# A hybrid two-layer trunk step on one core: wide routing, late modulation blocks, attention results by feature, split queries and keys

## The reference

```python
mc = split(silu(c_ctx) @ mod_w[l] + mod_b[l], 6)       # shift, scale, gate, shift2, scale2, gate2; ms: same with c
h  = rms_norm(x, norm1_w[l]) * (1 + scale) + shift
# layer 0: qa, ka, va, qb, ff, fb, ib, gb = split(h @ even_w_in)
#   8 query heads of 64 on 2 key heads; context tokens: dense attention with a sink;
#   latent tokens: rope, 128 cached keys and a band of +-128, with a sink
#   HGRN2 recurrence in both directions, 4 heads of 128; out = concat(a, o) @ even_w_out
# layer 1 (latent attention, 16 heads, 64 plain + 32 rotated dimensions):
#   q = rms_norm(h @ w_dq) @ w_uq; ckv, kr = h @ w_dkv; k = concat(ckv @ w_ukv[:, nope], kr)
#   out = softmax(q k / sqrt(96)) v @ w_o
x  = x + gate * out
h2 = rms_norm(x, norm2_w[l]) * (1 + scale2) + shift2
g  = softmax(h2 @ wg + bg); best group of 4
e  = h2 @ we + be within that group; top 2 of 8 experts, normalised, times the group's share
x  = x + gate2 * sum over the 2 experts of share * (silu(h2 Wg) * (h2 Wu)) Wd
```

## Time and profile before

| what | value |
|---|---|
| device time, median of 3 | 1198.02 us (1196.95 to 1198.96) |
| profiled execution: its time / its span | 1193.75 us / 1191.6 us |
| PE busy | 997.2 us (84%) |
| DVE busy | 478.0 us (40%) |
| ACT busy | 222.7 us (19%) |
| DMA | 320.71 MB, mean 269 GB/s |
| granted TensorE clock, mean | 0.927 of full |

### The profile page before, as it was taken

One profiled execution on the slowest core, in us unless ns is written; L12 is line 12 of the kernel. 1 busy time (PEld: TensorE's weight loads), 2 busy tenths in 40 slices (PEclk: granted clock), 3 DMA queues, 4 the chain that ended last, 5 costly groups with the idle time before them and its releaser, 6 DMA issues.

```text
span 1191.6 us, 15309 instructions
## 1 busy us (share of the span) xinstructions
PE 997.2 (84%) x6278; PEld 541.3 (45%) x6278; DVE 478.0 (40%) x1035; ACT 222.7 (19%) x487; POOL 107.9 (9%) x131
## 2 busy tenths in 40 slices
PE   4887897889999479988888698999995599988785
PEld 3544565447764433333333364566644333333242
DVE  1344445464442522322222626788324323321235
ACT  2134132223211210100000301322212101000002
POOL 0510010010000011111112000000000111111100
PEclk9888999987999679999899999999997699998998
DMA  9985547553675639999999721003366299999992
GB/s 357 358 336 212 212 146 286 213 199 111 215 285 227 256 128 417 425 424 425 426 426 348 254 81 40 1 1 142 157 266 265 88 415 424 423 425 424 425 404 97
DMA packets 84713, 320.71 MB, mean 269 GB/s; under 512 B 10155, under 2 KB 13755, under 8 KB 60832
## 3 DMA queue, kind: packets, MB, share of 16 engines
q1 hardware_dynamic: 69200, 288.86, 60.9%
q0 software_dynamic: 13664, 26.01, 6.3%
q10 hardware_dynamic: 1776, 4.81, 1.0%
HBM read 312.82 MB, written 26.53 MB: 285 GB/s over the span
## 4 chain that ended last, share of the span: by engine, by line
PE 59%; DMA 19%; DVE 11%; SPq 5%; ACT 3%; issue 3%; DVEq 0%; ACTq 0%; PEldq 0%; POOLq 0%
PE bank L773 26%; DMA ARENA<-in_moe_w_up 16%; PE bank L1077 11%; PE bank L1107 4%; SPq L574 3%; PE bank L924 3%; PE bank L799 3%; PE bank L945 2%; PE bank L1064 1%; PE bank L972 1%; DMA ARENA<-in_even_w_in 1%; SPq L577 1%; DMA ARENA<-in_mod_w 1%; PE bank L781 1%; PE bank L1087 1%
## 5 line engine op out<-in xcount | busy, mean ns | idle before, releaser
L1077 PE MATMUL bank<-ARENA 128*64 128x512 f32 x960 | 227.8, 630 | 35.1 <-DMA ARENA<-in_moe_w_up 33.5
L773 PE MATMUL bank<-ARENA,hT 128*128 128x512 f32 (+3 forms) x480 | 187.1, 549 | 6.1 <-DMA ARENA<-in_even_w_in 3.3
L1077 PEld LDWEIGHTS bank<-ARENA 128*64 128x64 f32 x960 | 76.5, 145 | 183.0 <-issue 180.7
L773 PEld LDWEIGHTS bank<-ARENA,hT 128*128 128x128 f32 x480 | 91.5, 193 | 94.1 <-issue 77.4
L1107 PE MATMUL bank<-ARENA 128*64 128x512 f32 x512 | 116.9, 599 | 15.1 <-ACT ARENA L1378 15.1
L1816 DVE TENSOR_TENSOR ARENA<-bank,ARENA 128x256 f32<-128x256 f32 x32 | 13.6, 424 | 248.1 <-ACT ARENA L1368 239.9
L673 POOL DMA_INDIRECT ARENA<-h_dram,ARENA x32 | 36.9, 1154 | 524.3 <-DVE ARENA L1805 308.8
L1368 ACT ACTIVATE ARENA<-bank 128x256 f32<-128x256 f32 x32 | 12.3, 383 | 377.1 <-PE bank L1077 348.1
L773 PE MATMUL bank<-hT,ARENA 128*128 128x384 f32 x192 | 68.0, 519 | 10.6 <-DVE hT L1971 5.2
L1831 DVE SCALAR_TENSOR_TENSOR GATE<-bank,ARENA,GATE 128x512 f32<-128x512 f32 x60 | 42.3, 747 | 84.5 <-PE bank L1107 84.5
L799 PE MATMUL bank<-ARENA,cond 128*32 128x128 f32 x1536 | 55.1, 303 | 21.2 <-DMA ARENA<-in_mod_w 15.7
(11 more groups left out here) (293 smaller groups left out, 1067.6 us busy)
## 6 DMA issues: line engine op xcount, KB each, us to landing
ARENA<-in_moe_w_down SPq DMA_DIRECT2D x32, 2048.0 KB, 31.0
ARENA<-in_moe_w_gate SPq DMA_DIRECT2D x30, 2048.0 KB, 27.2
ARENA<-in_moe_w_up SPq DMA_DIRECT2D x30, 2048.0 KB, 32.2
ARENA<-in_mod_w SPq DMA_DIRECT2D x24, 2048.0 KB, 11.4
ARENA<-in_even_w_in SPq DMA_DIRECT2D x6, 2048.0 KB, 8.7
y_dram<-ARENA POOLq DMA_DIRECT2D x2, 3072.0 KB, 14.1
ARENA<-y_dram SPq DMA_DIRECT2D x6, 1024.0 KB, 19.1
GATE<-mod_dram POOLq DMA_DIRECT2D x8, 512.0 KB, 5.2
```

Source lines behind the costliest of these rows:

```text
L773: last = nc.tensor.matmul(out, lhs(c), rhs(c), start=(c == 0), stop=(c == chunks - 1))
L1077: last = nc.tensor.matmul(banks[2 + i % 2][64 * e:64 * e + 64, :], XGT[:, c, 64 * e:64 * e + 64], w[:, e, :, c, :], start=(c == 0), stop=( ...
```

## The change

Five things change.

1. **Late modulation.** Block 18 is computed after the projection of tiles 0 and 1 of layer 0; 19 and 20 before the positions, 21 and 22 between positions and slots, 23 after the slots. SP loads 19 to 23 after the first two expert sets, and the third set only after all five are used. Blocks 18 to 23 are no longer in the attention.
2. **Attention results by feature.** The values are now the stationary operand (64 columns), two heads side by side, the turned probabilities stream (256 columns in layer 0, 128 in layer 1), and the result lies with features on partitions: ScalarE copies it straight into `hT`. `mixT` disappears in layer 1 and halves in layer 0 (the recurrence's part remains).
3. **Probabilities divided in place.** After the exponentials VectorE takes the reciprocal of the sums and multiplies the four heads' probabilities in place (`shares`); only then are they transposed. The division at the end goes.
4. **Split queries and keys in layer 1.** Plain part (64 rows, two heads in the two row halves) and rotated part (32 rows, four heads in the four row quarters) are separate matmuls that add up in one bank a head. ScalarE copies plain queries and keys, VectorE rotates four heads at once; the plain weights are laid out by ScalarE, the rotated ones by VectorE, eight heads at a time. Tile 0 of layer 1 uses four banks instead of one. ScalarE copies two of three transposed probability tiles in layer 1. In layer 0 the band masks follow the four heads' scores instead of each head's.
5. **Wide routing.** Loops over tiles and slots become single instructions with broadcast operands; positions take four matmuls instead of nine.

```diff
-MOD_IN_ATTENTION = {n: MODS - 6 + n for n in range(6)}
+TURNED_BY_SCALAR = (1, 2)
+MOD_IN_ATTENTION = {}
+MOD_LATE = 18
...
     if t == 0:
-        return [[0, 1, 2, 3]] if layer else [[0, 2], [1, 3]]
+        return [[0], [1], [2], [3]] if layer else [[0, 2], [1, 3]]
...
+            def late_modulations():
+                for m in (19, 20):
+                    load(blockno[("mod", m)])
+                    load_bias(m)
+                for m in (21, 22, 23):
+                    load(blockno[("mod", m)])
+                for m in (21, 22, 23):
+                    load_bias(m)
...
                 for i in range(PAIRS):
+                    if i == SETS - 1 and layer == 0:
+                        late_modulations()
                     if i == SETS - 1:
                         sp.wait_ge(block_used, first1 if layer == 0 else len(blocks))
                     load_pair(i)
...
+                        for h in range(4):
+                            half = slice(64 * (h % 2), 64 * (h % 2) + 64)
+                            nc.tensor.matmul(bank(("score", layer, n, h))[:, 0:nk], Q1[g % 2][half, h // 2, ts],
+                                             K1[g % 2][half, h // 2, ks], start=True, stop=False)
+                        for h in range(4):
+                            quarter = slice(RD * h, RD * h + RD)
+                            nc.tensor.matmul(banks[number[("score", layer, n, h)] % BANKS][:, 0:nk], QR1[g % 2][quarter, ts],
+                                             KRT[quarter, ks], start=False, stop=True).then_inc(bank_filled, 1)
...
                     if layer == 1 and t == 0 and g < 3:
                         queries_keys(g + 1)
+                    if n:
+                        results(n - 1)
...
+                    pe.wait_ge(shares_ready, 6 * layer + n + 1)
                     for i in range(len(kts)):
                         out = bank(("pT", layer, n, i))
...
-                    if n:
-                        results(n - 1)
...
+                def shares(n):
...
                     link(v.reciprocal(sp_[:, 20:24], sp_[:, 4:8]))
-                    b = filled(dve, ("pv", layer, n))
-                    emptied_by_me(v.tensor_tensor(MIX[:, t, 256 * g:256 * g + 256].rearrange("p (h e) -> p h e", h=4),
-                                                  b[:, 0:256].rearrange("p (h e) -> p h e", h=4),
-                                                  sp_[:, 20:24].unsqueeze(2).to_broadcast([P, 4, 64]), ALU.mult))
+                    for h in range(4):
+                        ins = v.tensor_scalar(pr[:, h, :], pr[:, h, :], sp_[:, 20 + h:21 + h], None, ALU.mult)
+                    ins.then_inc(shares_ready, 1)
...
                 for n, (g, t) in enumerate(groups):
+                    shares(n)
                     if n + 1 < len(groups):
                         maxima(n + 1)
...
+                def results(n):
+                    g, t = groups[n]
+                    b = filled(act, ("pv", layer, n))
+                    emptied_by_me(nc.scalar.activation(hT[:, 2 * g:2 * g + 2, t * P:(t + 1) * P],
+                                                       b[:, 0:2 * P].rearrange("p (j n) -> p j n", j=2), ACT.Copy))
...
                 project(layer, 1)
+                if layer == 0:
+                    late((), (18,))
...
             def assign(layer):
+                if layer == 0:
+                    late((18,), (19, 20))
                 new_input()
                 out = bank(("pos", layer))
...
+                if layer == 0:
+                    late((19, 20), (21, 22))
                 new_input()
                 out = bank(("slot", layer))
...
-                emptied_now(pe, ("slot", layer))
+                if layer == 0:
+                    late((21,), (23,))
+                emptied_now(pe, ("mod", 23) if layer == 0 else ("slot", layer))
...
-                for j in range(2 * NT):
-                    v.tensor_scalar(OHLO[:, j, :], ktab[:, 0:P], LOHI[:, 0, j:j + 1], None, ALU.is_equal)
-                    for half, row in enumerate((5, 3)):
-                        last = v.tensor_scalar(OHHI[:, j, half * PAIRS:(half + 1) * PAIRS], ktab[:, P:P + PAIRS],
-                                               LOHI[:, 1, j:j + 1], LOHI[:, row, j:j + 1], ALU.is_equal, ALU.mult)
+                v.tensor_tensor(OHLO, ktab[:, 0:P].unsqueeze(1).to_broadcast([P, 2 * NT, P]),
+                                LOHI[:, 0, :].unsqueeze(2).to_broadcast([P, 2 * NT, P]), ALU.is_equal)
+                pairs_of = OHHI[:, :, 0:PAIRS]
+                link(v.tensor_tensor(pairs_of, ktab[:, P:P + PAIRS].unsqueeze(1).to_broadcast([P, 2 * NT, PAIRS]),
+                                     LOHI[:, 1, :].unsqueeze(2).to_broadcast([P, 2 * NT, PAIRS]), ALU.is_equal))
+                link(v.tensor_tensor(OHHI[:, :, PAIRS:], pairs_of, LOHI[:, 3, :].unsqueeze(2).to_broadcast([P, 2 * NT, PAIRS]), ALU.mult))
+                feed(v.tensor_tensor(pairs_of, pairs_of, LOHI[:, 5, :].unsqueeze(2).to_broadcast([P, 2 * NT, PAIRS]), ALU.mult))
```

More of the change, by code:

```diff
@@ L143, in modulation, with late @@
     def modulation(n):
-        if turned_before(n) is not None:
+        if turned_before(n) is not None and n < MOD_LATE:
             add(("modT", turned_before(n)), "v")
         add(("mod", n), "v")
+    def late(turned, made):
+        for n in turned:
+            add(("modT", n), "v")
+        for n in made:
+            modulation(n)
     def project(layer, t):
@@ L195, in matmul_jobs @@
             attention(1)
[L196 to L197 removed]
+        if layer == 0:
+            for t in range(NT):
+                add(("mixT", t), "v")
         project(layer, 0)
         project(layer, 1)
+        if layer == 0:
+            late((), (18,))
         to_features("h2T", layer, 0)
@@ L931, in results @@
+                    if masked:
+                        far = 3 if t == 1 else 2
+                        for i in range(4):
+                            out = banks[number[("score", layer, n, i)] % BANKS]
+                            nc.tensor.matmul(out[:, (far - 1) * P:far * P], ident[:], band[:, t - 1, :],
+                                             start=False, stop=True).then_inc(bank_filled, 1)
                 def results(n):
@@ L983, in project @@
                         weights_arrived(pe, ("wout", layer, n))
-                for k in range(2):
-                    emptied_now(pe, ("mixT", layer, t, k))
+                if layer == 0:
+                    emptied_now(pe, ("mixT", t))
+                emptied_now(pe, ("pv", layer, len(attention_groups(layer)) - NT + t))
                 for n in range(2):
@@ L1014, in project_and_route @@
             def project_and_route(layer):
-                for t in range(NT):
-                    new_input()
-                    transposed("mixT", layer, t)
+                if layer == 0:
+                    for t in range(NT):
+                        new_input()
+                        readout_transposed(t)
                 project(layer, 0)
                 project(layer, 1)
+                if layer == 0:
+                    late((), (18,))
                 normalised(layer, 0)
@@ L1340, in exps @@
                         j = share[i].index(h)
+                        if layer == 1 and h == share[i][0]:
+                            go()
                         b = banks[number[("score", layer, n, i)] % BANKS]
@@ L1518, in _ @@
                     attention(1)
-                if layer == 0:
-                    act.wait_ge(stored, 16 * 4)
-                for t in range(NT):
-                    to_features("mixT", layer, t)
                 norm(0)
@@ L1641, in attention @@
                     pt = (PT0 if layer == 0 else PT1)
-                    for i in range(1, len(key_tiles(t))):
+                    if n:
+                        modulations(n - 1)
+                    for i in range(TURNED_BY_SCALAR[layer], len(key_tiles(t))):
                         b = filled(dve, ("pT", layer, n, i))
@@ L1928, in turned, with late @@
                     dve.wait_ge(modc_ready, 2 * l + (1 if b == 9 else 0) + 1)
+            def late(turns, made):
+                for m in turns:
+                    turned(m)
+                for m in made:
+                    modulation(m)
             def modulation(m):
-                if turned_before(m) is not None:
+                if turned_before(m) is not None and m < MOD_LATE:
                     turned(turned_before(m))
```

395 lines of the change are left out of this document (228 added, 167 removed).

## The result

The changed kernel took **1164.97 us** (median of 4 runs, 1163.14 to 1170.77) against 1198.49 of the kernel before on the same chip; the ratio is 0.9745, 95% interval 0.9709 to 0.9781. The forecast was 1165. Its profiled execution took 1164.32 us (span 1162.4), 29.4 less than that of before. A later set of runs gave 1167.82 against 1196.2 of the kernel before, ratio 0.9764 (0.9725 to 0.9804).

The account below looks back on a forecast made before the run. TensorE was taken to pace both attentions, DMA the pair stages, and neither the routing. Terms 2.3 - 22 - 1 - 8 - 4.8 = -33.5 us gave 1160.3 off the profiled time, 1164.5 off the median; forecast 1165, range 1144 to 1185.

Parts of the forecast that it names:

- Layer 0's attention: First scores to projection: 40.7 us TensorE work, 13 waits, 5 half clock, 58.7 against 80.8, so -22 us.
- Block 18 lies on the projections: +2.3: Layer 0's projections, all TensorE: block 18 computed there adds 2.3 us.
- Late blocks and set 3: -1: Layer 0's routing: its own gain (1 to 6.5 us) pays for a later third set; -3 to +3.5, taken as -1.
- the six modulations as a gain of the attention: Layer 0's attention: six modulations leave TensorE, 2.4 us each with turn and wait, 14.4 us.
- Layer 1's attention: -8: Layer 1's attention: TensorE saves 16 us, of which -8 us is taken, between +7 and -16.
- Results fall, 9.2 us: Layer 1's attention, TensorE: results fall from 2.7 to 1.55 us in eight full groups, 9.2 us.
- queries and keys 2.9: Layer 1's attention, TensorE: queries and keys of four heads fall from 11.64 to 10.9 us; four times 0.7 is 2.9.
- VectorE has room: Layer 1's attention: VectorE loses layouts and copies and has 96 us of 125 now, so it has room.
- Layer 1's routing: -4.8: Layer 1's routing: positions -2.2, one-hot rows -1.95, other loops -0.65 us; positions to slots about 6 us.
- The sum, -33.5: Whole kernel: 2.3 - 22 - 1 - 8 - 4.8 = -33.5 us; 1160.3 off the profiled time, 1164.5 off the median.
- the third (late blocks hold up the routing): Layer 0's routing: blocks 22 and 23 arrive 7 us late each, and the set with them: +14, 1179 us; chance 0.08.
- The second (the clock): Both attentions: clock falls and stays at 1.2 GHz; half of both stages low gives 1236 us; chance 0.06.

Follow-up runs that it names:

- Experiment 3: Changed kernel with block 18 computed in TensorE's wait for the readouts at the end of layer 0's attention: 1165.66 us, ratio 0.9745.
- experiment 9: Changed kernel with four late blocks, 18 in layer 0's attention, 19 in the readout wait, third set asked for earlier: 1159.35 us, ratio 0.9695.
- Experiment 1: Changed kernel with modulations 18 to 23 back in layer 0's attention and the third set loaded as before: 1161.58 us, ratio 0.9741.
- second profile: The changed kernel, nothing altered, run and profiled again beside the run of four late blocks: 1167.82 us, ratio 0.9764.
- experiment 8: Kernel before with only layer 1's results by feature and probabilities divided in place, no split queries and keys: 1203.99 us, ratio 1.0064.
- experiment 7: Changed kernel with layer 1's results back by token and eight transposes a tile, split and division kept: 1189.02 us, ratio 0.9934.
- experiments 3 to 5: Changed kernel with block 18 in the readout wait (1165.66 us), third set's gate and up weights asked for earlier (1162.98), or both (1159.83).

## Why the prediction was right, and where its steps were off

The total was right, and most prices were: scores, results, queries and keys, divisions, each within 0.15 us but for layer 0's scores (0.4). Layer 0's attention also came out by its terms and not only in its sum: of its 58.9 us TensorE is idle 11.5 (forecast 13), and 14.5 us at 1.2 GHz, taken as half lost, cost about 7 (forecast 5), which leaves about 40 of work (40.7). These points were not right:

- **"Block 18 lies on the projections: +2.3"** measured +4.7. The block itself is right (1.95 us and its wait). Missing was the clock: I let the 4.5 us of waits at the attention's end cost only themselves, and it fell there for 6.8 us. Experiment 3 fills the waits, and the fall is gone; in experiment 9 a fall of half that length is there all the same.
- **"Late blocks and set 3: -1"** measured +1.1 (routing -1.1, the expert stage +2.2), and the mechanism was there: the set is on its way at 404.15, behind block 23, and that sets when layer 1 starts. But the forecast counted the six modulations as a gain of the attention. Experiment 1 shows that they gain 6.2 and cost 10.0 behind it.
- **"Layer 1's attention: -8"** measured -10.1, -7.2 in the second profile. The sum is near; its parts do not add. "Results fall, 9.2 us" and "queries and keys 2.9" were priced as if each could be had alone. Experiments 8 and 7: each without the other, they cost 12 and 17 us. "VectorE has room" was true in the sum; by the rows of experiment 8 what counts is whether a long piece of VectorE's work stands ahead of what TensorE waits for.
- **"Layer 1's routing: -4.8"** measured -3.5. Positions to slots fall by 4.3 us (12.3 to 7.95), which is the two terms -2.2 and -1.95; "about 6" did not follow from them. The other loops' -0.65 did not come: from projection to positions it is 63.5 us, before the change 62.7.
- **The sum, -33.5.** The profiled executions differ by 29.4, the medians by 33.5. Off the profiled time the forecast would have been 1160.3, 4.7 us low; the median of before stood 4.3 above its profiled execution, and that made up for it. So the hit to within 0.1 us is luck; in the later set of runs the medians lie 28.4 apart.

Of the rivals, the third (late blocks hold up the routing) is near to what experiments 3 to 5 found, at a smaller price and by another way: for blocks 22 and 23 themselves TensorE waits only 0.31 and 0.33 us, and what comes late is the third set behind them. The second (the clock) did not decide, yet the sign that the forecast named for it, a clock of 0.5 inside either attention, is in every trace of the changed kernel: 3.4 us at 1.2 GHz in attention 1, 10.3 in the second profile, and 37.6 in experiment 7. The rule that I weighed against the change, from the Trainium skill (TensorE: Matmul & The Clock Gate, "A second HAM failure mode: psum-queue depth-cycling"), says of a kernel in bf16 that short idle times as TensorE goes round its banks make the clock swing. The trace agrees for experiment 8, where waits of 1.5 to 4.8 us and five falls come together; experiment 7 has 37.6 us at 1.2 GHz with no more idle time than the changed kernel, so idle time alone doesn't tell.

## What to carry to other kernels

Price the parts of a change together when one puts a new step on an engine's queue: ask what long work stands ahead of that step, and whether another part of the change takes it away. Where a stage has two limits side by side (here two transfers, each with its own distance to the next layer), what is gained on one of them can be given back, in part or whole, to the other; write down for each run which of the two is late. Work that fits in a wait of TensorE is worth more there than its own length, since a filled wait here also kept the clock in three profiles of four.

## What the hardware showed beyond that

- An indirect gather of tokens took 3.6 us from issue to use on a quiet DMA and 6.3 beside a 6.3 MB set of weights; the second one took 9.9 (9.6 with the first held).
- Eight matmuls of 32 rows by 384 columns on four row quarters took 0.93 us, against 1.56 us for eight of 64 rows on two halves.
- The same program runs attention 1 with one or with three short falls of the clock, and the stage is 2.9 us longer with three. Its six later runs spread over 13.0 us; what part of that is the clock is not shown.
